# The last row tiles of a two-layer decoder trunk: a store in column halves, and closing products and residual sum in column halves

## The reference

```python
for layer in range(DEPTH):                      # DEPTH = 2
    h = conv_sgu_mixer(x, ...) if layer % 2 == 0 else dilated_attention_mixer(x, ...)
    x = layer_norm(DN_ALPHA * x + h, ln_g[layer, 0], ln_b[layer, 0])
    x = layer_norm(DN_ALPHA * x + swiglu(x, ffn_w_gate[layer], ffn_w_up[layer], ffn_w_down[layer]),
                   ln_g[layer, 1], ln_b[layer, 1])
return x                                        # (1, 512, 1024)
# layer_norm: y = (x - mean) * rsqrt(var + 1e-5) * g + b over the 1024 channels of a position
```

## Time and profile before

| what | value |
|---|---|
| median of the runs | 1370.34 us (1370.0 to 1370.53, three runs) |
| the profiled execution's own time | 1370.82 us |
| its span in the trace | 1369.0 us |
| PE busy | 1355.4 us, 99% |
| last matmul starts | 1360.09 us |
| last transfer seen by SP | 1368.6 us |

### The profile page before, as it was taken

The page is one execution under the profiler, slowest core; times in us unless marked ns, Lnnn a source line. Parts: engine busy times, 40 slices in busy tenths (PEclk is TensorE's granted clock), DMA queues, the critical chain, the costliest instruction groups (busy, mean ns, idle before and its releaser), DMA issues.

```text
span 1369.0 us, 20672 instructions
## 1 busy us (share of the span) xinstructions
PE 1355.4 (99%) x8121; PEld 1208.5 (88%) x8121; DVE 887.1 (65%) x1122; ACT 615.3 (45%) x959; POOL 451.1 (33%) x218
## 2 busy tenths in 40 slices
PE   8999999999999999999999999999999999999997
PEld 7887899999988889888888888888889999998886
DVE  3997698888856355677433665724159888885445
ACT  4465555555542454333433434434255555554233
POOL 4785600000054454344443332444260000005443
PEclk9999999999999999999999999999999999999999
DMA  9323223343453323332442322254122334335321
GB/s 269 93 94 92 63 78 108 92 122 92 112 167 95 105 62 93 93 93 84 132 124 67 88 82 73 77 164 130 47 62 78 107 92 122 92 113 164 96 74 62
DMA packets 181961, 138.72 MB, mean 101 GB/s; under 512 B 8789, under 2 KB 162153, under 8 KB 181896
## 3 DMA queue, kind: packets, MB, share of 16 engines
q1 hardware_dynamic: 175272, 133.52, 33.3%
q10 hardware_dynamic: 6624, 4.29, 1.3%
HBM read 133.56 MB, written 4.24 MB: 101 GB/s over the span
## 4 chain that ended last, share of the span: by engine, by line
PE 97%; DVE 1%; DMA 1%; ACT 1%; SPq 0%; issue 0%; DVEq 0%
PE pq L940 10%; PE pq L939 10%; PE pq L937 10%; PE pq L712 9%; PE pq L714 9%; PE pq L713 9%; PE pq L734 8%; PE pq L735 8%; PE pq L736 8%; PE pq L1130 3%; PE pq L1131 3%; PE pq L1129 3%; PE pq L1108 1%; PE pq L1067 1%; PE pq L1080 1%; PE pq L1101 1%
## 5 line engine op out<-in xcount | busy, mean ns | idle before, releaser
L618 POOL TENSOR_TENSOR w_lo<-stage,w_hi 128x1024 fp32r<-128x1024 f32 x154 | 374.5, 2441 | 873.9 <-ACT w_hi L1201 873.8
L1201 ACT ACTIVATE w_hi<-stage 128x1024 fp32r<-128x1024 f32 x156 | 161.6, 1056 | 238.2 <-PE pq L736 164.8
L712 PE MATMUL pq<-xt_hi,w_hi 128*128 128x512 f32 (+1 forms) x624 | 228.4, 366 | 0.5 <-DVE xt_lo L1653 0.4
L714 PE MATMUL pq<-xt_hi,w_lo 128*128 128x512 f32 (+1 forms) x624 | 225.2, 361 | 0.0
L713 PE MATMUL pq<-xt_lo,w_hi 128*128 128x512 f32 (+1 forms) x624 | 225.1, 361 | 0.0
L940 PE MATMUL pq<-xt_hi,w_lo 128*128 128x256 f32 x632 | 178.9, 283 | 0.0
L939 PE MATMUL pq<-xt_lo,w_hi 128*128 128x256 f32 x632 | 178.9, 283 | 0.0
L937 PE MATMUL pq<-xt_hi,w_hi 128*128 128x256 f32 x632 | 178.8, 283 | 0.0
L712 PEld LDWEIGHTS pq<-xt_hi,w_hi 128*128 128x128 f32 x624 | 117.9, 189 | 19.5 <-DVE xt_lo L1653 1.2
L714 PEld LDWEIGHTS pq<-xt_hi,w_lo 128*128 128x128 f32 x624 | 117.8, 189 | 18.0
L937 PE MATMUL pq<-xs_hi,w_hi 128*128 128x256 f32 x472 | 133.6, 283 | 0.0
(11 more groups left out here) (261 smaller groups left out, 2808.4 us busy)
## 6 DMA issues: line engine op xcount, KB each, us to landing
stage<-in_od_w_qkv_dram SPq DMA_DIRECT2D x72, 512.0 KB, 3.9
stage<-in_ffn_w_gate_dram SPq DMA_DIRECT2D x44, 512.0 KB, 4.9
stage<-in_ffn_w_up_dram SPq DMA_DIRECT2D x44, 512.0 KB, 3.9
stage<-in_ffn_w_down_dram SPq DMA_DIRECT2D x44, 512.0 KB, 3.5
stage<-in_ev_w_in_dram SPq DMA_DIRECT2D x16, 512.0 KB, 5.7
stage<-in_ev_w_out_dram SPq DMA_DIRECT2D x8, 512.0 KB, 3.6
stage<-in_od_w_out_dram SPq DMA_DIRECT2D x8, 512.0 KB, 3.9
x_res<-in_x_dram SPq DMA_DIRECT2D x4, 512.0 KB, 6.2
```

What stands on the lines that cost most here:

```text
L618: pool.tensor_tensor(w_lo[slab % RING][:, :], w_stage[slab % RING][:, :], w_hi[slab % RING][:, :].bitcast(F32), ALU.subtract).then_inc(w_l ...
L712: pe.matmul(o, hi[:, k, :], x_hi, start=(k == 0), stop=False)
L714: last = pe.matmul(o, lo[:, k, :], x_hi, start=False, stop=(k == KD - 1))
L1201: act.activation(w_hi[slab % RING][:, :], w_stage[slab % RING][:, :], ACT.Copy).then_inc(w_hi_ready, 1)
```

## The change

Three things change, all at norm e = 3. Tile 2 is stored as two column halves, each as soon as POOL has added its half. PE's closing products of tile 3 go through all three slabs for columns 0 to 511, raise `acc_done`, and then do the same for columns 512 to 1023. DVE takes tile 3's residual sum in two instructions of 512 columns, each behind its own `acc_done`, whose two partial row sums (`half_sums`, a new buffer of two columns) are added and scaled by one `tensor_scalar`.

```diff
+        half_sums = sb("half_sums", [P, 2])
...
-            for i in range(SHIFT_TILES):
+            for i in range(SHIFT_TILES - 1):
                 sp.wait_ge(x_normed, 2 * (3 * SHIFT_TILES + i + 1))
                 sp.dma_start(out[0, i * P:(i + 1) * P, :], x_res[:, i, :]).then_inc(out_stored, 16)
+            for half in range(2):
+                cols, i = slice(half * 512, (half + 1) * 512), SHIFT_TILES - 1
+                sp.wait_ge(x_normed, 2 * (3 * SHIFT_TILES + i) + half + 1)
+                sp.dma_start(out[0, i * P:(i + 1) * P, cols], x_res[:, i, cols]).then_inc(out_stored, 16)
...
-            sp.wait_ge(out_stored, 16 * (TILES + 1))
+            sp.wait_ge(out_stored, 16 * (TILES + 2))
...
                 for i in range(TILES):
+                    if final_tile(e, i):
+                        for half in range(2):
+                            for j, (t_hi, t_lo) in enumerate(rows):
+                                last = tokens(slab + j, 512 * half, 512, pq[:, 2 * i + half, :], t_hi, t_lo, i, False, j == 2)
+                            last.then_inc(acc_done, 1)
+                        return
...
+            def final_in(e, i):
+
+                for half in range(2):
+                    cols = slice(half * 512, (half + 1) * 512)
+                    dve.wait_ge(acc_done, e * (TILES - 1) + i + half + 1)
+                    link.mark(dve.scalar_tensor_tensor(out=x_res[:, i, cols], in0=x_res[:, i, cols], scalar=ALPHA,
+                                                       in1=pq[:, 2 * i + half, :], op0=ALU.mult, op1=ALU.subtract,
+                                                       accum_out=half_sums[:, half:half + 1]))
+                link.wait()
+                dve.tensor_scalar(neg_mean[:, i:i + 1], half_sums[:, 0:1], half_sums[:, 1:2], -1.0 / D_MODEL, ALU.add,
+                                  ALU.mult).then_inc(row_summed, 1)
+
             def norm_in(e, i):
 
+                if final_tile(e, i):
+                    final_in(e, i)
+                    return
...
-                summed = halves(x_res[:, i, :]) if final_tile(e, i) else banks
-                link.mark(dve.scalar_tensor_tensor(out=summed, in0=halves(x_res[:, i, :]), scalar=ALPHA, in1=banks,
+                link.mark(dve.scalar_tensor_tensor(out=banks, in0=halves(x_res[:, i, :]), scalar=ALPHA, in1=banks,
```

## The result

| | before | after |
|---|---|---|
| median, 12 runs each | 1368.72 us (1368.5 to 1370.53) | 1372.83 us (1372.53 to 1375.03) |
| profiled execution, its span | 1370.82, 1369.0 | 1372.81, 1371.0 |

The account below looks back on a forecast made before the run. PE bounds the kernel, the bytes still to store its last 2.7 us. PE 0, store -0.60, split sum +0.2 hidden, product order 0, extra issue 0 gave -0.6: 1369.75 us from 1370.34, range for 8 of 10 1369.1 to 1370.8.

Parts of the forecast that it names:

- PE 0: PE's matmuls, whole kernel: none added or removed, the last still ends at 1360.48, so 0 us.
- The third rival: Buffers behind `half_sums` shift; PE or DVE slowed by 0.2% would give 1373; 8% together with anything else larger.
- Tile 2's store in halves: Final stores: first half moves before the last burst, which shrinks from 2.7 to 2.10 us, -0.60 us.
- the extra issue: SP's queue at the tail: one added store record of 0.34 us, delaying nothing, so 0.
- Tile 3's products by halves: PE's closing matmuls: columns 0 to 511 ready at 1358.44, but DVE arrives only at 1360.71, so 0.
- The split sum: DVE's residual sum of tile 3: +0.2 us (bounds +0.12 to +0.42), hidden by 0.4 us of cover.
- the `tensor_scalar`: DVE, adding tile 3's two half sums: stays one instruction of one column, 0.15 us, so 0 added.
- 1.35 to 1.65: Sign in the profile after: DVE's first half sum to negative mean takes this many us instead of 1.24.
- The end becoming DVE's: First rival, tail: split sum costs +0.42 and the last issue stays long; time 1370.0; 17%.
- The `tensor_scalar` held by POOL: Second rival, DVE's negative mean: blocked by POOL's addition, chain 1.07 or 2.3 us later, 1370.4 to 1371.6; 10%.
- The store not doing what it says: Fourth rival, final stores: tile 2's first half not issued until the second is ready, time stays 1370.3; 5%.
- 0.95 for no change: Whole kernel's time: chance given to a result within 0.2% (2.7 us); faster 0.02, slower 0.03.

Follow-up runs that it names:

- the kernel with only the shift: Kernel before plus an unused 32-byte buffer ahead of the phases' buffers, no instruction changed: 1373.33 us, ratio 1.0032.
- the kernel with the half summed in the gap: Changed kernel, `half_sums` in spare constants columns, tile 3's first half summed in DVE's gap ahead of tile 2's gain: 1368.12 us, ratio 0.9992.

## Why the prediction was wrong

**The step that failed** is the term "PE 0" of the sum. The third rival had named what could upset it, that `half_sums` moves the buffers behind it, and had set that aside with the reason that matmuls of one shape have the same length whichever buffer they read (0.39 us from hr and xs). The observation was right and the conclusion wrong. All those buffers have distances from w that are multiples of 256 bytes, so the row compared only pairs of the fast kind and could say nothing about any other. The term measured +5.27 us, the net of 1342 matmuls that became slower by 5 to 7 ns each and 1416 that became faster by 2. So "no matmul is added or removed, so the change can act only behind PE's last matmul or on it" was wrong too: it held for the instructions and not for what they read. I had named a loss of 0.2% and 1373 for this rival and gave all such cases 8% together. That 1373 lies close to the measured 1372.83 is luck: the 0.2% was a supposed size from no row, and it was counted from a median 1.6 us above the later one.

**Tile 2's store in halves**: right. -0.60 forecast, -0.60 measured alone (8.93 to 8.33). The burst is 2.1 us long, as three pieces at the 2 KB rows' pace should be, and the extra issue costs nothing. Nor did a fixed part of 2.0 us come on top, which the prediction worked out as the price if such parts lay end to end. The section it took that figure from, the Trainium skill's "DMA: Bandwidth & Descriptors", section Anatomy of one DMA, describes transfers that GpSimd issues, while SP issues these.

**Tile 3's products by halves, worth 0 because DVE isn't there**: right for the kernel as forecast (8.94 with them alone). In the changed kernel the tail is 0.96 shorter and not 0.60. The other 0.35 is part of PE's own delay, seen from its end. In both kernels DVE begins with tile 0 when PE has finished it and then goes at its own pace, 4.4 us for tile 0 and 4.0 each for tiles 1 and 2, waiting for ACT and not for PE. The 54 products that PE still has for tiles 1 to 3 take 0.35 us longer at 0.2335 us than at 0.227, so DVE starts tile 3's sum 0.26 us after the last matmul's start instead of 0.62. The same shows in the kernel with only the shift, whose tail is 8.58.

**The split sum, +0.2 and hidden**: right, at the lower end. It measured +0.13 (addition to the chain at DVE's last instruction), inside the bounds of 0.12 and 0.42, and 0.00 at the end. Of that, 0.08 is the sums and 0.06 the `tensor_scalar`, which was put at 0. The sign "1.35 to 1.65" for the sums was missed: they take 1.32.

**The rivals.** The end becoming DVE's: no. The last issue takes 0.67 to 0.79 us in every kernel in which tile 2 is stored whole ahead of it, and 0.33 to 0.45 in the five in which tile 2 goes in halves. The split sum alone and the store alone show it:

```profile
L604 SPq DMA_DIRECT2D out_dram<-x_res x2: 431/574/717, 1362.8 to 1363.3; - x2
...
L607 SPq DMA_DIRECT2D out_dram<-x_res x2: 432/440/448, 1362.6 to 1363.1; - x2
```

So it depends on what is ahead of it in the queue; that a full queue is what holds it is still only my reading.

The `tensor_scalar` held by POOL: it didn't happen, and it wasn't put to the test either. The new instruction starts 0.05 us ahead of POOL and not behind it, and its 0.21 us is its length without POOL too: the same 0.21 stands in the kernel with the half summed in the gap, where POOL starts 0.45 us after its end. One column with a scalar from SBUF, started behind POOL, stands in no run. One column with a fixed factor isn't held: 0.15 at 150.21, and 0.15 in the kernel with only the shift, where it starts 0.06 us behind POOL. Of the rule quoted from the Trainium skill ("SBUF — State Buffer", section Who interferes with whom) the trace has a case that agrees, the four-column one that takes 0.82 and ends with POOL's instruction, and these one-column cases that don't follow it.

The store not doing what it says: no, its two issues are 1.2 us apart.

**The chances**: 0.95 for no change rested on the reach of a 9 us tail. A new allocation in the middle of the memory map reaches the whole kernel.

## What to carry to other kernels

A new buffer is an edit to every buffer allocated behind it. Before such a change is judged by its instructions, compare the addresses of PE's operands before and after, or put the new columns where nothing moves behind them (spare columns of an old buffer, or padded to a multiple of 256 bytes, which cost nothing in the run with 256). In a trace with an engine 100% busy, compare the mean length of each group and the number of instructions in a fixed stretch, not the busy share.

## What the runs showed of the hardware that I had not expected

The pace of float32 matmuls here depends on the distance in bytes between the two operands' addresses within a partition, and what is left of it after division by 256 is what showed. Counted from the kernel before, where all these distances are multiples of 256, 512-wide products take 227 ns from start to start, 233.5 with one operand moved by 32 or 64 bytes and 232.5 with 128; moves by 256 and 512 give 227 again, and so does a move of both by 32. Other distances, and a common move by anything but 32, were not tried. For 256-wide products it is the other way round, 120.0 before and 118.0 to 118.9 otherwise (118.3 with only w moved). The sign goes with the width and not with which operand is loaded, since the 512-wide products that load w became slower too. A layout that puts the up projections' operands off each other and the down projections' on would use both; it wasn't tried, and both stages share w and xs. Why the two widths differ in sign, and which reads meet, is open.
